# Latent attention with two heads in one pass, a residual kept in DRAM, and index keys on the raw input

## The chip, the cores and the metric

The kernel runs on one core of a Trainium2 chip. A core has five engines that run their own lists of instructions and wait for each other by semaphores: TensorE (PE, matmuls; its weight loads are listed as PEld), VectorE (DVE), ScalarE (ACT), GpSimd (POOL) and SyncE (SP, which only issues DMA here). The metric is the device time of one execution in microseconds (us); less is better.

## The reference, cut to what matters

Two blocks run one after the other on x of 512 tokens by 1024 features, in float32. The first holds an mLSTM, an attention whose keys are selected by an indexer, and a gated embedding. The second holds a state-space mixer (SSD), a latent attention of 16 heads, a gated sum of the two, and a feed-forward part. The change lies in the indexer's key projection, in the residual of the second block, and in the latent attention:

```python
u = rmsnorm(h, norm_in[i])
proj = u @ w_in[i]              # ix_q, ix_k (indexer) are columns of it
...
q = (rms_norm(q_a, q_a_norm_g) @ w_uq).reshape(b, l, MLA_HEADS, MLA_QK_DIM)       # 16 x (64 + 32)
kv = (rms_norm(kv_a, kv_a_norm_g) @ w_ukv).reshape(b, l, MLA_HEADS, MLA_NOPE + MLA_V_DIM)   # 16 x (64 + 64)
k_nope, v = jnp.split(kv, [MLA_NOPE], axis=-1)
k_rope = jnp.broadcast_to(k_rope_raw[:, :, None, :], (b, l, MLA_HEADS, MLA_ROPE))
k = jnp.concatenate([k_nope, k_rope], axis=-1)
q = rms_norm(q, q_norm_g)
k = rms_norm(k, k_norm_g)
...                             # the 32 rope features of q and k are rotated
s = jnp.einsum('bqhd,bkhd->bhqk', qb, k).astype(jnp.float32) * scale              # causal
p = jax.nn.softmax(s, axis=-1).astype(v.dtype)
o = jnp.einsum('bhqk,bkhd->bqhd', p, v)
...
g_ssd, g_mla = jnp.split(jax.nn.sigmoid(gates + gate_b[i]), 2, axis=-1)
x = x + (g_ssd * y_ssd + g_mla * y_mla) @ w_o[i]
```

## The kernel before, in words

Features lie on the 128 partitions and the 512 tokens on the free axis. Every dense product is made of three matmuls for each 128 by 128 part of a weight, because operands are split in a high and a low part (`column_tile`, L678 to L680: high by high, high by low, low by high; 512 columns each). Weights come in chunks of 512 KB, each of eight parts, through a ring of four: SP loads a chunk into `w_raw`, ACT makes `w_hi` of it (L1265), POOL makes `w_lo` (L569), PE uses both. The order of the work is written out by hand for each engine, and semaphores tie the engines together. There are eight PSUM banks of 512 columns.

*Index part.* PE projects the index queries (`idx_q`) from `xg`, the raw input times its gain, whose per-token scale is put in afterwards (`query_scaled` on DVE, L1950), then the index keys (`idx_k`) and the tile `small` from `u`, the normalised input. DVE makes `u_val` (L1956), ACT `u_hi` (L1320), DVE `u_lo` (L1875), eight parts of each.

*Before the SSD.* DVE turns `h_res` into the second block's input and residual in eight instructions (L2215), each of which raises `x2_ready`. ACT issues three small loads of constants (L1574), reads the tile `small2` out of PSUM (L1577) and starts the chain of the time steps (L1581 to L1584, two table loads in it), which DVE goes on with (L2236 on), ahead of the convolution's taps (L2223). PE needs the taps of earlier tiles for their PSUM banks to come free.

*Latent attention.* The list `heads` holds the units (head, query block ti), four to a head, in the order of heads. For unit n PE makes the logits of n+2 (`head_logits`, L1142 and L1143, ti+1 blocks of 128 columns), turns the probabilities of n (`head_turn`, L1151), and multiplies those of n-1 with v (`head_values`, L1161): the turned probabilities are the stationary operand (128 columns) and 64 columns of v move. DVE takes the maximum (L2390, L2391); ACT takes the exponential (`head_probs`, L1751) and copies the turned block (`head_turned`, L1759); DVE divides the product by the sum (`head_out`, L2397 and L2399) into `o_tok`, tokens on partitions, which PE turns back to features for each pair of heads (`back`, L1169), with a DVE copy (L2420). For the head after next PE projects queries and keys (`project_queries`, `project_keys`); ACT squares both (L1718, L1723); DVE makes the features (`head_features`, L2363 to L2372); PE sums the squares over features with a column of ones (`query_sums` L1110, `key_sums` L1119), ACT takes the root (`head_norms`, L1733), DVE the reciprocal, PE spreads the key scale over partitions (`key_spread`, L1128) and DVE multiplies (`head_keys`, L2385). Between all this PE works on a tile of the mixing gates for each head (`mix_gate`, eight parts), for which ACT takes a sigmoid (L1742). Exponential, sigmoid and root stand in different table sets, so ACT loads tables between them. The logits use banks 4 and 5, the turned blocks bank 6, the values bank 7, queries and both sums bank 1, keys and their spread bank 2, gates banks 0 and 3.

*After it.* ACT and DVE split the attention's output (`o_hi` L1787, `o_lo`), PE multiplies it with the output weights (`mla_out`, L699 on), then `mix_out` adds to `h_res`.

## Time and profile before

| | |
|---|---|
| runs, us | 1763.4, 1768.36, 1768.3; median 1768.3 |
| profiled execution, us | 1767.63, of which the span is 1765.8 |
| mean granted clock of TensorE | 0.985 |
| busy, share of the span | PE 96%, PEld 77%, DVE 59%, ACT 48%, POOL 36% |
| latent attention, from its first projections to the first matmul of `mla_out` | 1022.7 to 1305.3 |

Start times of the trace count from the start of the span. A matmul of four-byte type on data that is not split appears as two instructions, and neighbours of one line are drawn together as xN; a matmul's printed duration reaches beyond the start of the next one, so the cost of one is the distance between two starts. What stands in brackets is the idle time of the engine before an instruction and what ended it.

### The profile page before, as it was taken

To read this page: it belongs to the slowest core of one execution; us is meant where nothing else is said; L and a number is where in the kernel's file an instruction comes from. 1 tells how busy PE (TensorE), PEld (TensorE's weight loads), DVE (VectorE), ACT (ScalarE), POOL (GpSimd) and SP (SyncE) were. 2 spreads that over 40 slices of the span, in tenths; PEclk is the share of its full clock that TensorE was granted. 3 is DMA by queue.
4 is the path that set the end of the run, shared out by engine and by line. 5 is a ranking of instruction groups with operands and counts; after the bars stand their busy time and mean duration, and the time that the engine had idled before them with its cause. 6 is when DMAs were issued, how large, how long until landed. Compare 5 with 4: busy or idle time off the path is not lost.

```text
span 1765.8 us, 23111 instructions
## 1 busy us (share of the span) xinstructions
PE 1701.7 (96%) x8091; PEld 1356.3 (77%) x8091; DVE 1045.6 (59%) x1646; ACT 855.6 (48%) x1370; POOL 628.7 (36%) x275
## 2 busy tenths in 40 slices
PE   7999899999999899999999999999999999999999
PEld 5688677767788788776677878888878788888887
DVE  6499478677426767677787045555546556655200
ACT  5423366655435454666663246666663244444210
POOL 4244221232444244343453421221234244444442
PEclk9999899999999899999999999999999899999999
DMA  5223212121333133211112311111113233333331
GB/s 194 65 91 96 89 54 61 59 61 60 134 109 97 50 105 99 72 49 48 37 60 73 106 60 37 61 48 37 50 60 107 72 96 95 96 98 100 99 96 60
DMA packets 39834, 138.56 MB, mean 78 GB/s; under 512 B 4664, under 2 KB 5144, under 8 KB 39616
## 3 DMA queue, kind: packets, MB, share of 16 engines
q1 hardware_dynamic: 37600, 131.96, 24.0%
q10 hardware_dynamic: 2144, 5.39, 1.0%
q8 instruction: 58, 0.95, 0.2%
q14 instruction: 32, 0.26, 0.0%
HBM read 135.21 MB, written 2.12 MB: 78 GB/s over the span
## 4 chain that ended last, share of the span: by engine, by line
PE 77%; DVE 12%; ACT 6%; issue 4%; POOL 0%; DVEq 0%; ACTq 0%; POOLq 0%
PE bank L678 15%; PE bank L680 15%; PE bank L679 15%; PE bank L1249 4%; PE bank L1248 4%; PE bank L1247 4%; PE bank L1142 2%; PE bank L729 1%; PE bank L731 1%; PE bank L730 1%; PE bank L818 1%; PE bank L1073 1%; PE bank L1161 1%; PE bank L836 1%; ACT L1742 1%
## 5 line engine op out<-in xcount | busy, mean ns | idle before, releaser
L569 POOL TENSOR_TENSOR w_lo<-w_raw,w_hi 128x1024 fp32r<-128x1024 f32 x243 | 591.1, 2435 | 1098.5 <-ACT w_hi L1265 953.0
L678 PE MATMUL bank<-u_hi,w_hi 128*128 128x512 f32 x784 | 331.3, 423 | 5.9 <-DVE taps L2223 3.2
L1265 ACT ACTIVATE w_hi<-w_raw 128x1024 fp32r<-128x1024 f32 x199 | 209.2, 1055 | 214.8 <-PE bank L680 176.4
L680 PE MATMUL bank<-u_hi,w_lo 128*128 128x512 f32 x784 | 308.8, 394 | 0.0
L679 PE MATMUL bank<-u_lo,w_hi 128*128 128x512 f32 x784 | 308.2, 393 | 0.0
L678 PEld LDWEIGHTS bank<-u_hi,w_hi 128*128 128x128 f32 x784 | 148.9, 190 | 65.3 <-issue 29.5
L680 PEld LDWEIGHTS bank<-u_hi,w_lo 128*128 128x128 f32 x784 | 148.5, 189 | 32.4
L679 PEld LDWEIGHTS bank<-u_lo,w_hi 128*128 128x128 f32 x784 | 149.2, 190 | 28.4 <-issue 3.1
L1248 PE MATMUL bank<-u_lo,w_hi 128*128 128x512 f32 x320 | 124.5, 389 | 0.0
L1247 PE MATMUL bank<-u_hi,w_hi 128*128 128x512 f32 x320 | 124.5, 389 | 0.0
L1249 PE MATMUL bank<-u_hi,w_lo 128*128 128x512 f32 x320 | 124.5, 389 | 0.0
L1248 PEld LDWEIGHTS bank<-u_lo,w_hi 128*128 128x128 f32 x320 | 60.1, 188 | 12.6
L1247 PEld LDWEIGHTS bank<-u_hi,w_hi 128*128 128x128 f32 x320 | 60.1, 188 | 12.5
L1249 PEld LDWEIGHTS bank<-u_hi,w_lo 128*128 128x128 f32 x320 | 60.1, 188 | 12.4
L2510 DVE TENSOR_TENSOR h_res<-h_res,bank 128x512 f32<-128x512 f32 x8 | 5.5, 687 | 107.1 <-PE bank L680 107.1
L679 PE MATMUL bank<-act_lo,w_hi 128*128 128x512 f32 x176 | 68.5, 389 | 0.0
L678 PE MATMUL bank<-act_hi,w_hi 128*128 128x512 f32 x176 | 68.5, 389 | 0.0
L680 PE MATMUL bank<-act_hi,w_lo 128*128 128x512 f32 x176 | 68.5, 389 | 0.0
L2223 DVE SCALAR_TENSOR_TENSOR taps<-bank,vecs,taps 128x511 f32<-128x511 f32 (+2 forms) x72 | 53.8, 748 | 23.5 <-ACT taps L1619 21.8
L2474 DVE SCALAR_TENSOR_TENSOR ffn_g<-bank,vecs,ffn_g 128x511 f32<-128x511 f32 x22 | 16.5, 750 | 69.5 <-ACT ffn_g L1812 69.5
L678 PE MATMUL bank<-y_hi,w_hi 128*128 128x512 f32 x128 | 51.4, 402 | 3.1 <-DVE y_lo L1875 3.1
L2399 DVE TENSOR_SCALAR o_tok<-bank,x_cols 128x64 f32<-128x64 f32 x64 | 18.1, 284 | 60.8 <-PE bank L1161 60.3
(454 smaller groups left out, 3655.8 us busy)
## 6 DMA issues: line engine op xcount, KB each, us to landing
w_raw<-weights SPq DMA_DIRECT2D x243, 512.0 KB, 3.5
xt<-x_t SPq DMA_DIRECT2D x8, 256.0 KB, 6.2
hank<-bias_dram ACTq DMA_DIRECT2D x8, 256.0 KB, 3.1
xt<-x_t ACTq DMA_DIRECT2D x1, 2048.0 KB, 9.4
out<-h_res SPq DMA_DIRECT2D x8, 256.0 KB
p_val<-p_t ACTq DMA_DIRECT2D x1, 512.0 KB, 11.5
trig<-trig ACTq DMA_DIRECT2D x1, 256.0 KB, 3.9
vecs<-vecs ACTq DMA_DIRECT2D x1, 214.0 KB, 4.8
```

The lines of the kernel that those rows point to most:

```text
L569: pool.tensor_tensor(w_lo[:, j, :], w_raw[:, j, :], w_hi[:, j, :].bitcast(F32), ALU.subtract).then_inc(w_lo_ready, 1)
L678: pe.matmul(o, hi, xh, start=(i == 0), stop=False)
L679: pe.matmul(o, hi, xl, start=False, stop=False)
L680: mm = pe.matmul(o, lo, xh, start=False, stop=(i == n - 1))
L729: pe.matmul(o, xh, hi, start=(k == 0), stop=False)
L1142: pe.matmul(o[:, 0:W], q_s[:, h % 2, ti * P:W], k_s[:, h % 2, 0:W], start=True, stop=False)
L1247: pe.matmul(bank[j][:, :], hi, xh, start=(k == 0), stop=False)
L1248: pe.matmul(bank[j][:, :], hi, xl, start=False, stop=False)
L1249: mm = pe.matmul(bank[j][:, :], lo, xh, start=False, stop=(k == KD - 1))
L1265: act.activation(w_hi[:, c % RING, :], w_raw[:, c % RING, :], ACT.Copy).then_inc(w_hi_ready, 1)
L2223: ins = dve.scalar_tensor_tensor(acc[:, back:S], b[:, 0:S - back], w(n - 1 - back), acc[:, back:S], ALU.mult, ALU.add)
L2399: dve.tensor_scalar(o_tok[:, ti, h * VD:(h + 1) * VD], bank[7][:, 0:VD], x_cols[:, 3, n:n + 1], None, ALU.mult).then_inc(x_out, 1)
```

## The change

1. *Order of units.* `heads` goes over pairs p of heads, query blocks ti, and the two heads s of the pair: the units of two heads alternate. In the loops, i = n mod 8 is the place of a unit in its pair.
2. *Values.* `pair_values` takes both heads of a pair: v (64 columns) is the stationary operand, in the array's column half s, and 128 columns of turned probabilities move. The output lies with features on partitions in bank 7, so `back`, its copy and `o_tok` go; `o_raw` is copied once for each pair. The division by the sum goes ahead of the turn: `head_scaled` (DVE: reciprocal, and a multiplication of the probabilities in place) stands between `head_probs` and `head_turn`.
3. *Keys.* The 64 key features of both heads form one tile of 128 columns (three matmuls for a pair), ACT moves the second head's 64 weight columns beside the first's (a copy in `split_weights`), the key sums take two columns, the spread goes by column halves, and DVE adds the rope part (`key_sums_add`). All sums are now in bank 2, where the keys also are, so `query_sums` of the pair's first head waits until DVE has read the keys (`key_features`).
4. *Gates.* The sigmoid becomes a tanh, with a half in `y_ssd` and in the probabilities, and one added where the gate is used.
5. *Residual.* `h_res` (2 MB) is written to DRAM by ACT's queue after `x2_ready` has come eight times, and read back after the last values; `mix_out` waits for it (`h_back`). Its place in SBUF holds `probs_x` and `turned_x`, four buffers each.
6. *Index keys.* `idx_k` is computed on `xg` as `idx_q` is, and DVE scales it; `u_val` takes the scale from PSUM (bank 5) instead of `r_in` in SBUF.

```diff
+                if k == 6:
+                    pe.wait_ge(ones_ready, 1)
+                    token_sums(lambda k: sq[:, 0, :], lambda k: sq[:, 1, :])
+            column_tile(q2, of_xg, part=(0, 1))
             spread_scale(0, 5)
-            column_tile(q2, of_xg, part=(4, 8))
+            column_tile(q2, of_xg, part=(1, 8))
             column_tile(q3, of_xg)
+            column_tile(st["idx_k"][0], of_xg)
...
-            column_tile(st["idx_k"][0], of_u, 0)
-            column_tile(st["small"][0], of_u)
+            column_tile(st["small"][0], of_u, 0)
...
+            def project_keys(p):
...
+                hi, lo = (w[:, c % RING, 2 * P:3 * P] for w in (w_hi, w_lo))
+                o = bank[2][:, :]
+                pe.matmul(o, hi, kn_hi[:, :], start=True, stop=False)
+                pe.matmul(o, hi, kn_lo[:, :], start=False, stop=False)
+                pe.matmul(o, lo, kn_hi[:, :], start=False, stop=True).then_inc(dense_done, 1)
...
             def query_sums(h):
-                pe.wait_ge(head_sq, 2 * h + 1)
-                pe.wait_ge(dve_freed, st["head_q"][h]["freed"][1])
+                p, s = divmod(h, 2)
+                pe.wait_ge(head_sq, 3 * p + (3 if s else 1))
+                if not s:
+                    pe.wait_ge(head_sq, 3 * p + 2)
+                    pe.wait_ge(dve_freed, st["head_k"][p]["freed"][1])
...
+                    mm = pe.matmul(bank[2][:, s * NT + ti:s * NT + ti + 1], sq_q[:, ti * P:(ti + 1) * P],
+                                   ones[0:QK, 0:1], start=True, stop=True)
+                mm.then_inc(head_sums, 1)
...
+            def key_spread(p):
+                pe.wait_ge(r_qk_ready, p + 1)
...
-                                   stop=True)
+                    for s in range(2):
+                        q = 2 * (NT + c) + s
+                        mm = pe.matmul(bank[2][64 * s:64 * s + 64, c * P:(c + 1) * P],
+                                       r_qk[:, p % 2, q:q + 1].broadcast_to([P, NOPE]), ident[:, :], start=True,
+                                       stop=True)
                 mm.then_inc(rk_spread, 1)
...
-                pe.wait_ge(x_probs, n + 1)
+                pe.wait_ge(x_scaled, n + 1)
...
+            def pair_values(k):
+                p, ti = divmod(k, NT)
+                pe.wait_ge(x_turned_out, 2 * k + 2)
+                if p and ti == 0:
+                    pe.wait_ge(x_out, p)
                 for j in range(ti + 1):
-                    mm = pe.matmul(o, turned_x[n % 2][:, j * P:(j + 1) * P], v_tok[:, j, h * VD:(h + 1) * VD],
-                                   start=(j == 0), stop=(j == ti))
+                    for s in range(2):
+                        h = 2 * p + s
+                        mm = pe.matmul(bank[7][64 * s:64 * s + 64, ti * P:(ti + 1) * P],
+                                       v_tok[:, j, h * VD:(h + 1) * VD],
+                                       turned_x[:, (2 * k + s) % 4, j * P:(j + 1) * P], start=(j == 0), stop=(j == ti))
                 mm.then_inc(x_sum, 1)
...
+                if more and i == 0:
+                    project_query(2 * p + 2)
+                    project_keys(p + 1)
+                if more and i == 2:
+                    project_query(2 * p + 3)
+                if more:
+                    column_tile(st["mix_gate"][2 * p + 1 + i // 4], of_u2, part=(i % 4 * 2, i % 4 * 2 + 2))
+                else:
+                    column_tile(st["mix_gate"][2 * p + 1], of_u2, part=(i, i + 1))
+                if more and i == 1:
+                    query_sums(2 * p + 2)
+                    key_sums(p + 1)
+                if more and i == 3:
+                    query_sums(2 * p + 3)
+                if more and i == 4:
+                    key_spread(p + 1)
...
-                if n:
-                    head_values(n - 1)
...
+                if n and n % 2 == 0:
+                    pair_values(n // 2 - 1)
+            pair_values(len(heads) // 2 - 1)
...
+            act.wait_ge(x2_ready, KD)
+            act.dma_start(h_dram, h_res[:, :, :].rearrange("p a b -> p (a b)")).then_inc(h_spilled, 16)
...
-            act.activation(sq_k[NOPE:QK, :], small2[NOPE:QK, :], ACT.Square).then_inc(krope_sq, 1)
+            act.wait_ge(h_spilled, 16)
...
-                act.activation(gm[:, h % KD, :], bank[t["bank"]][:, :], ACT.Sigmoid,
-                               bias=vec("gate_b", h)).then_inc(act_freed, 1)
+                act.activation(gm[:, h % KD, :], bank[t["bank"]][:, :], ACT.Tanh, bias=half_b[:, h:h + 1],
+                               scale=0.5).then_inc(act_freed, 1)
...
+                if more and i == 0:
+                    query_squares(2 * p + 2)
+                    key_squares(p + 1)
+                if more and i == 2:
+                    query_squares(2 * p + 3)
                 head_turned(n)
-                if ti == 1 and h:
-                    after(st["mix_gate"][h - 1])
-            act.wait_ge(o_turned, KD - 1)
+                if more and i == 2:
+                    after(st["head_q"][2 * p + 3])
+                if more and i == 3:
+                    head_norms(p + 1)
+                    after(st["mix_gate"][2 * p + 1])
+                if more and i == 7:
+                    after(st["mix_gate"][2 * p + 2])
+            act.wait_ge(x_sum, len(heads) // 2)
+            act.dma_start(h_res[:, :, :].rearrange("p a b -> p (a b)"), h_dram).then_inc(h_back, 16)
...
+                act.activation(o_hi[:, i, :], o_raw[:, i, :], ACT.Copy).then_inc(hi_ready, 1)
...
-                return dve.scalar_tensor_tensor(u_val[:, i % 2, :], xt[:, i, :], vec("norm_in", i), r_in[:, :],
+                if i in (4, 6):
+                    query_scaled(i // 2)
+                return dve.scalar_tensor_tensor(u_val[:, i % 2, :], xt[:, i, :], vec("norm_in", i), bank[5][:, :],
...
+            t = st["idx_k"][0]
+            dve.wait_ge(dense_done, t["full"])
+            free(dve.tensor_tensor(ik[:, :], bank[t["bank"]][:, :], r_in[:, :], ALU.mult))
...
+            def key_features(p):
...
+                dve.wait_ge(head_sq, 3 * p + 2)
+                if p:
+                    dve.wait_ge(k_ready, 2 * p)
+                free(dve.tensor_scalar(k_raw[:, :], bank[2][:, :], k_gain[:, :], None, ALU.mult))
...
+            def head_scaled(n):
...
+                W = (heads[n][1] + 1) * P
                 dve.wait_ge(x_probs, n + 1)
                 link(dve.reciprocal(x_cols[:, 3, n:n + 1], x_cols[:, 2, n:n + 1]))
-                dve.wait_ge(x_sum, n + 1)
-                dve.tensor_scalar(o_tok[:, ti, h * VD:(h + 1) * VD], bank[7][:, 0:VD], x_cols[:, 3, n:n + 1],
-                                  None, ALU.mult).then_inc(x_out, 1)
+                dve.tensor_scalar(probs_x[:, n % 4, 0:W], probs_x[:, n % 4, 0:W], x_cols[:, 3, n:n + 1], 0.5,
+                                  ALU.mult, ALU.mult).then_inc(x_scaled, 1)
...
+                head_scaled(n)
+                if p and i == 1:
+                    dve.wait_ge(x_sum, NT * p)
+                    dve.tensor_copy(o_raw[:, p - 1, :], bank[7][:, :]).then_inc(x_out, 1)
+                if more and i == 4:
+                    head_scales(p + 1)
                 if n + 2 < len(heads):
                     head_max(n + 2)
...
+                if more:
+                    if i == 0:
+                        query_features(2 * p + 2, 0)
+                        query_features(2 * p + 2, 1)
+                    if i == 1:
+                        key_features(p + 1)
+                    if i == 2:
+                        key_sums_add(p + 1)
+                        query_features(2 * p + 3, 0)
+                    if i == 3:
+                        query_features(2 * p + 3, 1)
+                    if i in (4, 5):
+                        head_keys(2 * p + i - 2)
+                if i == 2 and 2 * p < KD:
+                    gate_used(2 * p)
+                if i == 5 and 2 * p + 1 < KD:
+                    gate_used(2 * p + 1)
             dve.wait_ge(gates_used, KD)
+            dve.wait_ge(x_sum, len(heads) // 2)
```

On ACT, between the end of the first block and the SSD stage, the list before reads (`u_hi` is the split input, `small_140` the tile `small2`):

```order
L1320 ACTIVATE u_hi<-val_f 128x512 [waits val_ready] x8
L1574 DMA one_hot<-one_hot 96x32
L1574 DMA trig<-trig 128x512
L1574 DMA tri_b<-tri_b 128x128
L1577 ACTIVATE small_140<-bank,vecs 128x512 [waits dense_done]
L1265 ACTIVATE w_hi<-w_raw 128x1024 [waits dense_done,w_landed0]
L1581 ACTIVATE r_t_149<-small_140 32x512 [waits act_freed]
```

and after the change:

```order
L1354 ACTIVATE u_hi<-val_f 128x512 [waits val_ready] x8
L1600 DMA h_dram<-h_res 128x4096 [waits x2_ready]
L1603 DMA one_hot<-one_hot 96x32
L1603 DMA trig<-trig 128x512
L1603 DMA tri_b<-tri_b 128x128
L1606 ACTIVATE small_140<-bank,vecs 128x512 [waits dense_done]
L1299 ACTIVATE w_hi<-w_raw 128x1024 [waits dense_done,w_landed0]
L1610 ACTIVATE r_t_149<-small_140 32x512 [waits act_freed]
```

One DMA with a wait has come in ahead of all the others; nothing else moved.

On PE, in the latent attention, the sums of squares stood in the middle of a head like this (`qn`: the split latent queries, `u`: those of the gates, `squares_f`: the identity):

```order
L1110 MATMUL bank<-ones,sq_q 128x1 [waits dve_freed,head_sq]
L1110 MATMUL bank<-ones,sq_q 128x1 x3
L678 MATMUL bank<-u_hi,w_hi 128x512 [waits w_lo_ready]
L679 MATMUL bank<-u_lo,w_hi 128x512
L680 MATMUL bank<-u_hi,w_lo 128x512
L1119 MATMUL bank<-ones,sq_k 128x1 [waits head_sq]
L1119 MATMUL bank<-ones,sq_k 128x1 x3
L1151 MATMUL bank<-squares_f,probs_x 128x128 [waits x_turned_out,x_probs]
L1161 MATMUL bank<-v_tok,turned_x_180 128x64 [waits x_out,x_turned_out]
L1161 MATMUL bank<-v_tok,turned_x_180 128x64 x3
```

and stand after the change in the second unit of a pair, behind that pair's gate parts:

```order
L694 MATMUL bank<-u_hi,w_hi 128x512
L695 MATMUL bank<-u_lo,w_hi 128x512
L696 MATMUL bank<-u_hi,w_lo 128x512
L1148 MATMUL bank<-ones,sq_q 128x1 [waits dve_freed,head_sq]
L1148 MATMUL bank<-ones,sq_q 128x1 x3
L1156 MATMUL bank<-in_half,sq_k 128x2 [waits head_sq]
L1156 MATMUL bank<-in_half,sq_k 128x2 x3
L1190 MATMUL bank<-squares_f,probs_x 128x128 [waits x_turned_out,x_scaled]
L1181 MATMUL bank<-k_s,q_s 128x384 [waits x_probs]
L1182 MATMUL bank<-tri_b,squares_b 128x128
```

The sums of the first query and of the keys now follow each other without a matmul of the gates between them, the first of them waits for DVE's reading of the keys, and the turn behind them waits for `x_scaled` (DVE) where it waited for `x_probs` (ACT).

On ACT, around the roots, before (one head):

```order
L1751 ACTIVATE probs_x,x_cols<-bank,x_cols,r_qk 128x256 [waits x_turn,x_max]
L1733 ACT_TABLE_LOAD [waits rk_spread,x_probs]
L1733 ACTIVATE r_qk<-bank,vecs 128x4 [waits head_sums]
L1734 ACTIVATE r_qk<-bank,vecs 128x4
L1759 COPY turned_x_179<-bank 128x128 [waits x_sum,x_turn]
L1742 ACT_TABLE_LOAD
L1742 ACTIVATE gm<-bank,vecs 128x512 [waits dense_done]
L1751 ACT_TABLE_LOAD [waits x_turn]
L1751 ACTIVATE probs_x,x_cols<-bank,x_cols,r_qk 128x384 [waits x_max]
```

and after (fourth to fifth unit of a pair):

```order
L1787 COPY turned_x<-bank 128x256 [waits x_turn]
L1759 ACT_TABLE_LOAD [waits k_sums_in]
L1759 ACTIVATE r_qk<-bank,vecs 128x8 [waits head_sums]
L1760 ACTIVATE r_qk<-r_qk,vecs 128x8
L1299 ACTIVATE w_hi<-w_raw 128x1024 [waits dense_done,w_landed0]
L1769 ACT_TABLE_LOAD
L1769 ACTIVATE gm<-bank,half_b 128x512 [waits dense_done]
L1779 ACTIVATE probs_x,x_cols<-bank,x_cols,r_qk 128x384 [waits x_turn,x_max]
L1787 COPY turned_x<-bank 128x384 [waits x_sum,x_turn]
```

Two of the three table loads are still there, now once for a pair of heads; the load between gate and exponential is gone; a weight copy stands between root and gate.

## Rows read from the trace of the kernel before

**Rows 1.** The page, its first part: busy time, share and count of each engine.

```profile
PE 1701.7 (96%) x8091; PEld 1356.3 (77%) x8091; DVE 1045.6 (59%) x1646; ACT 855.6 (48%) x1370; POOL 628.7 (36%) x275
```

**Rows 2.** Windows of the latent attention: us, busy (count), PEclk, DMA share, GB/s.

```profile
1022.70:1038.40 15.70, 15.70 (x83) 13.38 (x82) 7.16 (x11) 7.70 (x13) 2.39 (x1) 1.00 0.17 61
1038.40:1304.80 266.40, 260.83 (x1556) 214.50 (x1554) 145.49 (x377) 178.71 (x340) 57.14 (x24) 0.97 0.15 47
1042.20:1049.00 6.80, 5.85 (x22) 4.59 (x23) 2.49 (x6) 3.80 (x8) 4.23 (x2) 0.62 0.43 131
```

**Rows 3.** Groups of instructions by line and form, 1000 to 1320 us.

```profile
L1751 ACT ACT_TABLE_LOAD x17 | 21.8, 1283 | 0.3
```

**Rows 4.** Timeline of PE inside one head: start, us, engine, line.

```profile
1178.88 0.39 PE L680 MATMUL bank<-u_hi,w_lo 128*128 128x512 f32 x1
1179.11 0.95 PE L1119 MATMUL bank<-ones,sq_k 96*128 96x1 f32 x8
1179.92 0.31 PE L1151 MATMUL bank<-squares_f,probs_x 128*128 128x128 f32 x1
1180.07 1.00 PE L1161 MATMUL bank<-v_tok,turned_x 128*128 128x64 f32 x8
1180.91 0.65 PE L1142 MATMUL bank<-k_s,q_s 96*128 96x512 f32 x1
```

**Rows 5.** Timeline of PE in the SSD stage, column halves.

```profile
740.97 0.38 PE L969 MATMUL bank<-squares_b 128*128 128x512 bf16 x1
741.28 0.41 PE L979 MATMUL bank<-stack_a,one_hot 96*64 96x512 bf16 x2
741.66 0.51 PE L1073 MATMUL bank<-weight_a,xdt 128*64 128x128 f32 x3
```

**Rows 6.** Waits of PE, 1020 to 1320 us.

```profile
PE bank L1110 <- DVE q_s L2368: 2.2, 2, 1.6
```

**Rows 7.** Timeline of DVE: the features of one head.

```profile
1173.64 0.73 DVE L2363 TENSOR_SCALAR q_s<-bank,vecs 64x512 f32<-64x512 f32 x1
...
1176.70 0.74 DVE L2372 TENSOR_SCALAR rope<-bank,vecs 64x512 f32<-64x512 f32 x1
```

**Rows 8.** Timeline of ACT: a table load, a gate, a weight copy.

```profile
1164.20 1.28 ACT L1742 ACT_TABLE_LOAD   x1
1165.50 0.69 ACT L1742 ACTIVATE gm<-bank,vecs 128x512 f32<-128x512 f32 x1
...
1173.89 1.05 ACT L1265 ACTIVATE w_hi<-w_raw 128x1024 fp32r<-128x1024 f32 x1
```

**Rows 9.** Timeline of POOL in the index part.

```profile
41.24 2.52 POOL L569 TENSOR_TENSOR w_lo<-w_raw,w_hi 128x1024 fp32r<-128x1024 f32 x1 [2.24 <-ACT w_hi L1265]
```

**Rows 10.** Timeline of DVE in the index part.

```profile
40.18 0.75 DVE L1956 SCALAR_TENSOR_TENSOR u_val<-xt,vecs,r_in 128x512 f32<-128x512 f32 x1
...
41.57 2.75 DVE L1956 SCALAR_TENSOR_TENSOR u_val<-xt,vecs,r_in 128x512 f32<-128x512 f32 x1
```

**Rows 11.** One line, L2012, DVE: duration min/median/max.

```profile
L2012 DVE TENSOR_SCALAR relu<-score,top x3: 420/487/2485, 142.2 to 155.9; 128x256 f32<-128x256 f32 x1, 128x384 f32<-128x384 f32 x1, 128x512 f32<-128x512 f32 x1
```

**Rows 12.** Timeline of PE in the index part.

```profile
44.97 0.50 PE L678 MATMUL bank<-u_hi,w_hi 128*128 128x512 f32 x1 [2.29 <-DVE u_lo L1875]
...
48.67 0.63 PE L678 MATMUL bank<-u_hi,w_hi 128*128 128x512 f32 x1
```

**Rows 13.** Timeline of ACT before the SSD stage.

```profile
587.37 1.65 ACTq L1574 DMA_DIRECT2D trig<-trig  x1
...
591.69 0.69 ACT L1577 ACTIVATE small<-bank,vecs 128x512 f32<-128x512 f32 x1 [4.06 <-PE bank L704]
```

**Rows 14.** Timeline of DVE at the same place.

```profile
592.81 5.36 DVE L2215 SCALAR_TENSOR_TENSOR h_res<-h_res,vecs,bank 128x512 f32<-128x512 f32 x8 [4.39 <-PE bank L654]
...
609.12 2.97 DVE L2223 SCALAR_TENSOR_TENSOR taps<-bank,vecs,taps 128x511 f32<-128x511 f32 x4
```

**Rows 15.** Timeline of PE at the same place.

```profile
611.49 0.50 PE L678 MATMUL bank<-u_hi,w_hi 128*128 128x512 f32 x1 [2.39 <-DVE taps L2223]
```

More of the change, by code:

```diff
@@ L133, in make_plan @@
     plan = Plan()
-    for name, n, kt, reader in (("idx_q", 4, KD, "D"), ("idx_k", 1, KD, "A"), ("small", 1, KD, "A"),
+    for name, n, kt, reader in (("idx_q", 4, KD, "D"), ("idx_k", 1, KD, "D"), ("small", 1, KD, "A"),
                                 ("att_q", 4, KD, "A"), ("att_k", 4, KD, "A")):
@@ L469, in weight @@
             return weights2[h // 2 % 2][:, h % 2, :]
-        heads = [(h, ti) for h in range(XH) for ti in range(NT)]
+        heads = [(2 * p + s, ti) for p in range(XH // 2) for ti in range(NT) for s in range(2)]
         up = st["up"]
@@ L1256, in _ @@
             next_hi, steps, evs, sqs, his = [0], [0], [0], [0], [0]
+            pair_chunks = [t["parts"][0][0] for t in st["head_k"]]
             def split_weights(done):
@@ L1359, in _ @@
             token_std(bank[4][:, 0:NT], 0)
-            for i, t in enumerate(st["idx_q"]):
+            for t, first, end in zip(st["idx_q"] + st["idx_k"], (0, 0, 3, 5, 7), (0, 3, 5, 7, KD)):
                 tile_done(t)
                 after(t)
-                if i:
-                    n = (3, 2, 3)[i - 1]
-                    k = (0, 3, 5)[i - 1]
-                    high_parts(lambda i: u_hi[:, k + i, :], lambda i: u_val[:, (k + i) % 2, :], n)
+                high_parts(lambda i: u_hi[:, first + i, :], lambda i: u_val[:, (first + i) % 2, :], end - first)
             act.wait_ge(bias_dot, 1)
@@ L1376, in _ @@
             act.sem_inc(bias_ready, 1)
-            t = st["idx_k"][0]
-            tile_done(t)
-            act.copy(ik[:, :], bank[t["bank"]][:, :]).then_inc(act_freed, 1)
-            after(t)
             t = st["small"][0]
@@ L2442, in fuse @@
+            low(bank[7][:, :], o_hi[:, KD - 1, :], o_lo[:, KD - 1, :])
             def fuse(i):
```

371 lines of the change are left out of this document (182 added, 189 removed).

## The prediction

> **What bounds the kernel now.** I read the page's first part, then the latent attention by windows, then PE's waits there, then the timelines of single heads. PE is busy 96% of the span, the other engines 36 to 59% [rows 1], so an edit pays by the PE time that it removes and costs by the PE wait that it adds. The latent attention takes 15.7 us of preparation and 266.4 us of loop, together 282.1, with PE idle 5.6 of it and a mean granted clock of 0.97 in the loop [rows 2]. PE's only long waits there are for DVE's query features, 2.2 us in two [rows 6]. After the first of them the clock stood at 0.62 for 6.8 us, half speed for most of it [rows 2]; so an idle moment of PE costs more than its length. At 260.8 busy us, 3% of clock is 7.8 us at most; I take 6.8. Full-clock PE work of the stage is then 282.1 - 5.6 - 6.8 = 269.7.
>
> **PE work that goes.** Keys: three 512-column matmuls for a pair instead of six, 24 fewer at 0.23 each (1178.88 to 1179.11) [rows 4], 5.5 us. Key sums: 4 columns of 4 matmuls for each pair instead of 8 matmuls; eight instructions take 0.81 (1179.11 to 1179.92) [rows 4], so 8 x 0.81 = 6.5, with the change-over 7.2. Spread: 64 matmuls of 96 stationary columns become 64 of 64 columns in alternate halves. Values: 160 matmuls, 320 instructions, at 0.84 for eight (1180.07 to 1180.91) [rows 4] = 33.6; their number stays, but neighbours now go to different column halves. Two 512-column products in two column halves both stand at 741.28, and the next instruction starts 0.38 later, where one alone takes 0.23 and two would take 0.46 [rows 4, 5]. So halves run beside each other, and a change of form costs some 0.09 going in (0.31 from 740.97 to 741.28) and coming out. The floor is then half the price: values 33.6/2 and spread (priced as the sums, 16 x 0.81 = 13) 13/2, a gain of 16.8 + 6.5, and 1.8 for the short units. The other end of the range is no overlap at all: gain nothing, and 0.1 in and 0.1 out of each group. I take the overlap, as the nearest row in form shows it. Switches: five groups for a pair (four of values, one of spread) and the last, 41 x 0.19 = 7.8 back. Turning back goes: 32 matmuls, at 0.11 each (0.81 for eight) [rows 4] 3.5. Sum: 5.5 + 7.2 + 25.1 + 3.5 - 7.8 = 33.5 less, 236.2 left.
>
> **Waits that come.** Worked through one pair of the new order with the old durations, PE meets five. (a) In the second unit `query_sums` stands behind logits, query, keys and two gate parts, about 7.0 us after the pair's start, and needs the keys read by DVE. ACT has 3.6 us ahead of the squares' end (a turned block, the weight copy 1.05 [rows 8] with the small copy that it follows now, gate, exponential, square), DVE then four query operations, 3.06 us together [rows 7], `head_scaled`, a maximum of 0.65, the copy of the values and the key operation of 0.74 [rows 7], 5.5 in all: 9.1, so PE waits 2.1. Behind the waiting instruction stand the key sums, the turn and the logits; ACT's next roots depend on the sums. (b) In the fourth unit, 0.4, the query features behind one multiplication. (c) In the fifth, 0.5, the spread behind roots and reciprocal. (d) In the same place 1.0: ACT has turned block, table load 1.29, roots, weight copy 1.05, table load, gate 0.69 and exponential in a row [rows 3, 8] before PE's logits buffer comes free. (e) 0.3 for the first values of a unit. Together 4.3 for each of seven pairs, 30.1, and 3.5 in the preparation, where four of these chains run for the first time: 33.6. Table loads fall from 48 (17 in the row shown, 16 and 15 in two like it, 1.28 each [rows 3]) to 15; ACT waited for PE, not PE for ACT, so this pays nothing by itself.
>
> So the stage is 236.2 + 33.6 = 269.8 before the clock. The clock: before, one wait of 1.65 us was followed by the fall [rows 2, 6]; now seven pairs have one of 2.1 beside eight one-column sums. If each fall costs 1.4 us and the preparation 2, the sum is 11.5, between 4 (falls in a few pairs) and 18 (all as deep as the one shown). I take 11.5: 281.3, **0.8 less** than now.
>
> The trace shows 1.30 us from the start of a table load to the activation behind it [rows 8]. The Trainium skill, "ScalarE: Activation LUTs", section "What ACT_TABLE_LOAD costs", adds a drain of some 1.38 us to every load of 1.28. By it wait (d) would be 2.7 us longer for each pair, 19 us in all; the time would be 1794. The trace has no such gap, so the row stands in the sum and that case gets no chance.
>
> **The spill.** ACT's queue now waits for eight `x2_ready` ahead of the other loads and ahead of `small2`. DVE's eight instructions run 592.81 to 598.17; `small2` is read at 591.69 today [rows 13, 14]. It would be read behind 598.17, one issue of 0.34, and the three constants' (1.65 for the longest [rows 13], 2.4 together): 601.1, which is 9.4 later; 8.0 if the long issue shrinks in a quiet queue. The time-step chain behind it (ACT two table loads, DVE until 609.12 [rows 14]) hides nothing: DVE follows ACT closely, then the taps start at 609.12, and PE waits for them already, 2.39 us until 611.49 [rows 15]. So PE starts again at 620.9 and, after 12 us of idling, at half clock for a while, 2 us. Nothing in the SSD stage catches up, since PE had no other wait over 0.2 us in the next 100 us. **11.4 more**, 8 to 14. The transfer itself has hundreds of us.
>
> **The index part.** DVE's `u_val` takes 2.75 us instead of 0.75 where POOL's `w_lo` runs [rows 9, 10]; PE waits 2.29 for it at 44.97, and `small` starts at 48.67 at half clock [rows 12]. Now `idx_k` needs no `u`, and seven of eight parts can be ready behind it; `u_val` with one operand in SBUF shouldn't stretch. `small` would start at 44.4 or so at full clock: 4.2 + 0.8 = **5.0 less**, 3.5 to 6.
>
> **Behind the attention.** `mla_out` starts behind the last values (`x_sum`), the issue of the 2 MB read, and one copy of 0.6, where today most copies lie under the last unit: **1.2 more**. The read itself is needed a whole `mla_out` later.
>
> **Sum.** -0.8 + 11.4 - 5.0 + 1.2 = 6.8 on the profiled execution of 1767.6, which is 0.7 below the median of the runs; I give **1775.0 us** against 1768.3, 0.4% more. Under 0.3% (5.3 us) nothing can be told from no change here.
>
> **The rivals.**
> *A, the forecast*, 1766 to 1784. Chance 0.48.
> *B, the saving reaches the end*: waits (a) to (e) are half of what I worked out (an operation order one step better than mine, or DVE's 59% load [rows 1] leaving room), and the clock stays up. Then 15 us of waits and 9 of clock are saved: 1751, 1743 to 1760. For it: DVE and ACT both lose work. Against it: the sums now wait for DVE's reading of a shared bank. It decides when (a) is below 1 us. Chance 0.22.
> *C, the spill is hidden*: DVE ends its eight instructions sooner or the time steps have slack that I don't see. 11 less, 1764. Against it the 2.39 us wait at 611.49 [rows 15]. Chance 0.08.
> *D, column halves don't overlap* for four-byte operands; the product in rows 5 is of two-byte ones, and four-byte ones in alternate halves (L1073 in the same rows) start 0.05 apart in some places of the SSD stage and 0.11 in others. Of the 3.1 us that the overlap gives for each pair (25.1 / 8) 2.2 would be missing, the rest shortens waits: seven times, 1790. Chance 0.10.
> *E, POOL holds up `head_scaled`*. That operation goes from SBUF to SBUF, as L2012 does, which took 0.42 to 0.49 us and once 2.49 [rows 11]; before, the division read PSUM. It now stands between exponential and turn, three 512 KB chunks for a pair, each with 2.5 us of POOL [rows 9]. If one in each pair is caught fully, 2.0 us, and the 0.4 of wait (b) hides a part, 1.6 reach PE, 11 in seven pairs: 1786. The Trainium skill, "SBUF — State Buffer", section "Who interferes with whom", says the same of such operations: they take a port pair that GpSimd shares, and one fully blocks the other. Chance 0.12.
>
> **How the numbers follow.** Faster: B and the low ends of A and C, 0.30. Within 0.3%: a third of A, half of C, 0.20. Slower: the rest of A, D and E, 0.50. The likeliest case's own range is 1766 to 1784; since cases of both signs hold the chance, the range reaches from 1746 in B to 1790 in D and E, and leaves about 2 in 10 out.
>
> **What would show it.** `small2` read at about 601 and an idle PE of 10 us or more at 609 to 621; PE without its 2.3 us wait at 45; the stage from the first `head_q` to `mla_out` within 4 us of 282; two in-pair waits of 1 to 2 us behind DVE's key operation and ACT's gate, and PEclk at 8 there; pairs of L1202 instructions 0.05 to 0.06 apart (D: 0.11); `head_scaled` at 0.3 to 0.5 us (E: 2 us and more). The prediction is wrong if the attention stage is under 270 us, or if the spill's delay doesn't arrive at PE.

## The result, and the profile after

The changed kernel takes 1785.2 us (1784.8 to 1785.9, 4 runs) against 1765.9 (1760.4 to 1768.4, 4 runs): ratio 1.0114, 95% interval 1.0087 to 1.0142. It is 1.1% slower: the side that was forecast and inside the range (1746 to 1790), but 19 us more instead of 7, and a microsecond outside what the likeliest case allowed (1766 to 1784).

The page of the changed kernel, span, busy shares and the row of the clock, against [rows 1]:

```profile
span 1783.3 us, 22683 instructions
PE 1687.7 (95%) x7960; PEld 1323.6 (74%) x7979; DVE 1069.8 (60%) x1667; ACT 809.7 (45%) x1320; POOL 629.1 (35%) x275
...
PEclk9999899999998899999999989999999999999999
```

PE is busy 14 us less and the span is 17.5 longer, so what was removed is not what decided the time. (The profiled executions, whose spans are compared from here on, differ by 17.5 us, the medians by 19.4.) Four marks of the two traces tell where it goes. ACT's last `u_hi` ahead of the SSD starts at 581.59 instead of 587.00: 5.4 sooner. PE goes on behind the taps at 616.50 instead of 611.49 [rows 15]: 5.0 later, so 10.4 were lost in between. The first query of the latent attention starts at 1029.5 instead of 1022.7, 6.8 later; `mla_out` starts at 1324.2 instead of 1305.3, 18.9 later; the end is 17.5 later. So: index part -5.4, spill (the write of the residual) +12.2, latent attention +12.1, behind it -1.4.

From the first mark on, ACT's queue before the SSD (DMA issues of ACT are marked ACTq), against [rows 13], then PE at the same place, against [rows 15]:

```profile
581.59 0.63 ACT L1354 ACTIVATE u_hi<-val_f 128x512 fp32r<-128x512 f32 x1 [0.75 <-DVE val_f L2254]
593.60 0.33 ACTq L1600 DMA_DIRECT2D h_dram<-h_res  x1
...
595.42 1.29 ACTq L1603 DMA_DIRECT2D tri_b<-tri_b  x1
596.76 0.69 ACT L1606 ACTIVATE small<-bank,vecs 128x512 f32<-128x512 f32 x1 [14.54 <-issue]
```

```profile
600.97 0.47 PE L694 MATMUL bank<-u_hi,w_hi 128*128 128x512 f32 x1 [1.91 <-POOL w_lo L585]
616.50 0.79 PE L694 MATMUL bank<-u_hi,w_hi 128*128 128x512 f32 x1 [9.85 <-DVE taps L2267]
```

ACT sits idle for 14.5 us in front of `small2`. At PE this comes out as two waits: 9.85 for the taps, and 1.91 for a weight chunk whose `w_hi` stands behind `small2` on ACT.

The latent attention by windows, whole and for two pairs of heads (columns as in [rows 2]), then PE's waits in it, against [rows 6]:

```profile
1029.48:1324.18 294.70, 265.01 (x1529) 196.46 (x1528) 175.27 (x401) 140.51 (x302) 59.37 (x25) 0.93 0.15 48
```

```profile
1085.63:1122.11 36.48, 33.05 (x189) 24.55 (x188) 21.19 (x51) 17.11 (x37) 7.12 (x3) 0.91 0.14 44
1122.11:1157.65 35.54, 31.61 (x190) 23.23 (x189) 23.28 (x51) 17.11 (x37) 7.11 (x3) 0.95 0.15 46
```

```profile
PE bank L1148 <- DVE k_raw L2424: 11.6, 7, 1.8
PE bank L1181 <- ACT probs_x L1779: 9.1, 9, 1.2
PE bank L1190 <- DVE probs_x L2463: 2.2, 6, 0.5
PE bank L745 <- DVE v_tok L1959: 1.7, 1, 1.7
PE bank L1166 <- DVE r_qk L2438: 1.5, 7, 0.4
PE bank L1181 <- DVE k_s L2447: 1.5, 2, 0.9
PE bank L715 <- ACT o_hi L1831: 1.3, 1, 1.3
PE bank L1202 <- ACT turned_x L1787: 0.7, 1, 0.7
```

A pair of heads takes 34 to 37 us, where two heads took 33.3 to 34.7 before. The waits come to 29.6 us. PE around one of the longest waits, in the pair from 1122.11:

```profile
1134.91 0.40 PE L696 MATMUL bank<-u_hi,w_lo 128*128 128x512 f32 x1
1137.13 1.02 PE L1148 MATMUL bank<-ones,sq_q 96*128 96x1 f32 x8 [1.82 <-DVE k_raw L2424]
1138.01 1.03 PE L1156 MATMUL bank<-in_half,sq_k 128*128 128x2 f32 x8
...
1140.94 0.63 PE L695 MATMUL bank<-qn_lo,w_hi 128*128 128x512 f32 x1
1141.37 0.63 PE L696 MATMUL bank<-qn_hi,w_lo 128*128 128x512 f32 x1
```

Some two microseconds behind the idle time the matmuls slow down: a 512-column one costs 0.43 instead of 0.23 (1140.94 to 1141.37). This is the lower of the clock's two levels, 1.2 instead of 2.4 GHz, here for 3.4 us. In three pairs it lasts twice as long, behind the same wait of 1.8 us. Two windows inside such stretches, the first in the pair from 1085.63:

```profile
1101.60:1108.30 6.70, 6.70 (x21) 5.23 (x22) 0.84 (x3) 1.31 (x4) 0.00 (x0) 0.50 0.01 2
1139.15:1142.45 3.30, 3.30 (x9) 2.12 (x8) 0.84 (x3) 0.82 (x3) 0.00 (x0) 0.50 0.00 0
```

I call such a stretch a fall of the clock. In the stage there are six falls of 3.4 us and three of 6.8, 41.0 us at half speed together, in which half, 20.5 us, is lost. In the kernel before there were one of 6.8 and two of 3.4: 13.7 us, 6.8 lost.

### The profile page after: what moved, and what is told of

It reads as the page before. It is cut to its first block, busy times and chain, and to the rows that moved or that the text cites. A ratio compares the mean times of both kernels' runs of the same rounds, so it can differ in the third digit from the quotient of the medians.

```text
span 1783.3 us, 22683 instructions
## 1 busy us (share of the span) xinstructions
PE 1687.7 (95%) x7960; PEld 1323.6 (74%) x7979; DVE 1069.8 (60%) x1667; ACT 809.7 (45%) x1320; POOL 629.1 (35%) x275
## 4 chain that ended last, share of the span: by engine, by line
PE 74%; DVE 15%; ACT 6%; issue 4%; POOL 0%; ACTq 0%; DVEq 0%; POOLq 0%
PE bank L694 15%; PE bank L696 14%; PE bank L695 14%; PE bank L1278 4%; PE bank L1277 4%; PE bank L1279 4%; PE bank L1181 2%; PE bank L745 1%; PE bank L746 1%; PE bank L747 1%; PE bank L835 1%; PE bank L1090 1%; PE bank L853 1%; ACT w_hi L1299 1%; PE bank L1190 1%
## 5 line engine op out<-in xcount | busy, mean ns | idle before, releaser
L694 PE MATMUL bank<-u_hi,w_hi 128*128 128x512 f32 x776 | 327.0, 421 | 12.5 <-DVE taps L2267 10.6
L1787 ACT COPY turned_x<-bank 128x128 f32<-128x128 f32 (+3 forms) x64 | 27.3, 426 | 114.0 <-PE bank L1190 114.0
L1279 PEld LDWEIGHTS bank<-u_hi,w_lo 128*128 128x128 f32 x320 | 60.1, 188 | 12.5
L2410 DVE TENSOR_SCALAR q_s<-bank,vecs 64x512 f32<-64x512 f32 x16 | 11.9, 743 | 82.8 <-ACT sq_q L1748 82.8
L2454 DVE TENSOR_REDUCE x_cols<-bank 128x1 f32<-128x128 f32 (+3 forms) x64 | 31.4, 490 | 50.4 <-PE bank L1182 49.6
```

Source lines behind the costliest of these rows:

```text
L694: pe.matmul(o, hi, xh, start=(i == 0), stop=False)
L1279: mm = pe.matmul(bank[j][:, :], lo, xh, start=False, stop=(k == KD - 1))
L1787: act.copy(turned_x[:, n % 4, 0:W], bank[6][:, 0:W]).then_inc(x_turned_out, 1)
L2454: link(dve.reduce_max(x_cols[:, 0, n:n + 1], bank[4 + n % 2][:, 0:(ti + 1) * P], AX_X))
```

## The experiments

Twelve kernels ran, each beside runs of the kernel before on the same chip. Times are medians; ratios are to the kernel before, with 95% intervals.

**1. The index part alone**, on the kernel before (part 6 of the change):

```diff
             column_tile(q3, of_xg)
+            column_tile(st["idx_k"][0], of_xg)
...
-            column_tile(st["idx_k"][0], of_u, 0)
```

> The kernel before with the index part of the change alone. If the index part is worth what the trace of the changed kernel suggests (everything behind it starts 5.4 us sooner), the time falls by 5 to 5.5 us, to 1760.5, with no PE wait at 45 us. If that gain is given back where PE next waits for a chunk of weights or a DVE chain, it falls by less than 2 us.

1758.9 against 1763.9, ratio 0.9973 (0.9958 to 0.9987): 5 us less, where the interval allows 2 to 7. PE has no wait left between 26 and 100 us but one of 0.4. The part does what was forecast.

**2. The residual alone**, written and read back, on the kernel before:

```diff
+            act.wait_ge(x2_ready, KD)
+            act.dma_start(h_dram, h_res[:, :, :].rearrange("p a b -> p (a b)")).then_inc(h_spilled, 16)
...
+            act.dma_start(h_res[:, :, :].rearrange("p a b -> p (a b)"), h_dram).then_inc(h_back, 16)
...
+            dve.wait_ge(h_back, 16)
```

> The kernel before with the residual written out and read back where the change does it, and nothing else. Theory: the wait on ACT's queue alone costs 10 to 12 us (1776 to 1778), with PE idle some 10 us behind the taps. Rival: the wait costs little by itself and the long idle time in the changed kernel comes from the earlier arrival of PE (index part); then the time rises by 4 to 6 us only.

1777.3, ratio 1.0069 (1.0051 to 1.0087): 12 us more by the ratio. PE's waits at the place, in this kernel:

```profile
PE bank L681 <- DVE taps L2230: 9.8, 1, 9.8
PE bank L681 <- POOL w_lo L572: 1.9, 1, 1.9
```

They are those of the changed kernel to a tenth, so neither the index part nor the attention has a share in them.

**3. The changed kernel with the residual written later**, behind the time-step chain:

```diff
-            act.wait_ge(x2_ready, KD)
-            act.dma_start(h_dram, h_res[:, :, :].rearrange("p a b -> p (a b)")).then_inc(h_spilled, 16)
...
             act.activation(r_t2[:, :], r_t2[:, :], ACT.Ln, bias=1.0).then_inc(dt_log, 1)
+            act.wait_ge(x2_ready, KD)
+            act.dma_start(h_dram, h_res[:, :, :].rearrange("p a b -> p (a b)")).then_inc(h_spilled, 16)
```

> The changed kernel with the write of the residual issued behind the time-step chain. The output is unchanged. Theory: 9 to 11 us come back (1785.2 to 1775), the wait behind the taps is 2 to 3 us again. Rival (something else holds the time steps): less than 3 us. Whatever stays above 1766 - 5 = 1761 is then the attention's, 12 to 14 us.

1772.6, ratio 1.0049 (1.0031 to 1.0067), 0.65% below the changed kernel. The wait behind the taps is 2.2 us. So the place of one DMA issue on a queue cost over 11 us; the transfer, which is made here too, costs nothing that shows.

**4. The changed kernel with the keys read first** by DVE:

```diff
                         query_features(2 * p + 2, 0)
                         query_features(2 * p + 2, 1)
-                    if i == 1:
                         key_features(p + 1)
```

> The changed kernel with DVE's reading of the keys moved ahead of a scaling, a maximum and the copy of the values. Theory that waits and the clock falls behind them make the attention slow: the wait for k_raw (11.6 us in 7) falls below 2 us, and falls of the clock go with it; 10 us from the waits and 7 x 1.7 from the clock, 1763 to 1770. Rival, that the clock falls for another reason (one-column sums in one block): the waits go but the falls stay, 1775 to 1777. Rival, that the next wait takes its place (the exponential, 9.1 us in 9): 1780 and more.

1763.7, ratio 0.9996 (0.9983 to 1.0008): 21 us below the changed kernel, the time of the kernel before. The latent attention of this kernel:

```profile
1029.00:1301.20 272.20, 253.55 (x1529) 188.65 (x1528) 174.64 (x401) 140.38 (x302) 59.27 (x25) 0.97 0.17 52
```

The wait for `k_raw` is gone; the others stay as they were (9.1, 2.2, 1.7 and so on; only the one for `r_qk` falls from 1.5 to 1.2). The stage is 22.5 us shorter. Of this 11.0 is idle time (29.7 falls to 18.7), and 11.5 is busy time for the same matmuls, which is the clock: 17.1 us at half speed instead of 41.0. So half of what a 1.8 us wait cost came behind it.

Two of the five falls that are left stand behind the one-column sums with no wait over 0.3 us ahead of them. One of them, and a window of the kernel before with such a fall:

```profile
1129.83 1.03 PE L1156 MATMUL bank<-in_half,sq_k 128*128 128x2 f32 x8
...
1132.00 0.63 PE L695 MATMUL bank<-qn_lo,w_hi 128*128 128x512 f32 x1
1132.43 0.63 PE L696 MATMUL bank<-qn_hi,w_lo 128*128 128x512 f32 x1
```

```profile
1146.30:1149.50 3.20, 3.20 (x7) 1.74 (x8) 1.19 (x3) 3.16 (x4) 0.00 (x0) 0.50 0.00 0
```

**5. The sums apart**, in the changed kernel: a gate part between query sums and key sums.

```diff
-                if more:
+                if more and i == 1:
+                    column_tile(st["mix_gate"][2 * p + 1], of_u2, part=(2, 3))
+                elif more:
...
                     query_sums(2 * p + 2)
+                    column_tile(st["mix_gate"][2 * p + 1], of_u2, part=(3, 4))
                     key_sums(p + 1)
```

> The changed kernel (no repair) with one gate part moved between the query sums and the key sums, so that the one-column matmuls behind the wait no longer stand in one block; the wait for the keys stays and grows by 0.7 in each of seven pairs. Theory that idleness makes the clock fall: the falls (40.9 us at half speed) stay, the time is that of the changed kernel or up to 5 us more. Rival, that the block of one-column matmuls is what lets it fall: the falls go, 8 to 12 us less.

1795.6, ratio 1.0175 (1.0161 to 1.0189), 11 us above the changed kernel. Its latent attention:

```profile
1027.36:1333.20 305.84, 272.14 (x1530) 201.82 (x1528) 173.17 (x401) 140.54 (x302) 59.41 (x25) 0.91 0.15 46
```

The wait for `k_raw` grew from 11.6 to 16.1 us and the falls from 41.0 to 58.0 us at half speed, though the one-column matmuls no longer stand in a block. So in these kernels the falls grow and shrink with the idle time, and parting the sums doesn't take them away. Idle time isn't their only cause: the falls without a wait in number 4 and in the kernel before stand behind such sums, and what makes those was not tested. The time went up by more than the 5 us of either theory, because I had not let the falls grow with the wait.

**6. Three repairs together**: late residual, keys first, and on ACT the fifth unit's gate and its weight copy behind the exponential.

```diff
-                if more and i == 4:
-                    mix_gate(2 * p + 1)
                 if n + 1 < len(heads):
                     head_probs(n + 1)
+                if more and i == 4:
+                    after(st["mix_gate"][2 * p + 1])
...
+                if more and i == 4:
+                    mix_gate(2 * p + 1)
                 if more and i == 3:
                     head_norms(p + 1)
-                    after(st["mix_gate"][2 * p + 1])
```

> The changed kernel with three repairs: the residual written behind the time steps, the keys read first, and ACT's gate and weight copy of the fifth unit behind the exponential. If the first two add up (12.7 and 21.5 us, from the same changed kernel's 1785.2), 1751; the third takes most of the 9.1 us for which PE waits for the exponential, so 1743 to 1748. If that wait only moves (to the turned blocks or the next gate's bank), 1750 to 1752. Against 1764 of the kernel before: ratio 0.988 to 0.993.

1757.0, ratio 0.9958 (0.9944 to 0.9971), above what was expected of two repairs alone. PE's wait for the exponential fell from 9.1 to 1.5, and one for the scaling rose from 2.2 to 12.9. DVE and POOL there, in this kernel:

```profile
1134.28 0.16 DVE L2463 RECIPROCAL x_cols<-x_cols 128x1 f32<-128x1 f32 x1
1134.48 2.61 DVE L2464 TENSOR_SCALAR probs_x<-probs_x,x_cols 128x384 f32<-128x384 f32 x1
```

```profile
1134.49 2.38 POOL L585 TENSOR_TENSOR w_lo<-w_raw,w_hi 128x1024 fp32r<-128x1024 f32 x1 [5.23 <-ACT w_hi L1299]
```

The moved weight copy lets POOL start as the scaling does, in almost every pair: 11 of 64 scalings take over 1 us, where it was 4 in the changed kernel, and 0.42 is usual for 384 columns.

**7. The two repairs without the third.**

> The changed kernel with two repairs: the residual written behind the time steps, and the keys read first. If the two add up (12.7 and 21.5 us) 1751, ratio 0.992 to the kernel before. The kernel with the third repair as well measured 1757; if that third one was harmful because it put POOL's weight copies on the scaling (11 scalings stretched instead of 4), this kernel is 3 to 6 us faster than it and has 4 stretched scalings. Rival, that the two repairs don't add up: 1757 here too.

1753.3, ratio 0.9937 (0.9918 to 0.9957). Five scalings over 1 us. The two repairs bring 1.8% in ratio against the changed kernel, where alone they bring 0.65 and 1.2: they add up. That the third was harmful is likely from this but not certain, since the intervals of numbers 6 and 7 overlap (0.9944 to 0.9971 against 0.9918 to 0.9957).

**8. Two repairs, and the gate alone behind the exponential** (the weight copy stays where it was):

```diff
-                if more and i == 4:
-                    mix_gate(2 * p + 1)
                 if n + 1 < len(heads):
                     head_probs(n + 1)
...
+                if more and i == 4:
+                    mix_gate(2 * p + 1)
                 if more and i == 3:
                     head_norms(p + 1)
                     after(st["mix_gate"][2 * p + 1])
```

> The two repairs (late residual, keys first; 1753.3, ratio 0.9937), and of the third only the gate's tanh moved behind the exponential and the turned block; the weight copy stays between root and table load. The exponential comes 0.6 us sooner, when POOL's w_lo (from 0.1 us after the weight copy, 2.4 us long) is all but over. Theory that only the moved weight copy made the third repair harmful: the waits for the exponential fall from 8.9 to 3 to 5 us, no more than 6 scalings take over 1 us, the time falls by 3 to 6 us to 1747 to 1750. Rival, that any earlier exponential meets POOL: 10 or more stretched scalings, 1754 or more.

1749.1 (1744.1 to 1753.1), ratio 0.9919 (0.9899 to 0.9938): the fastest kernel of the study whose output is whole, 0.8% under the kernel before. Its waits:

```profile
PE bank L1181 <- ACT probs_x L1779: 4.9, 9, 1.2
PE bank L1190 <- DVE probs_x L2463: 2.7, 7, 0.5
```

Five scalings over 1 us. This kernel and that of number 6 differ in the weight copy's place alone, and their intervals lie apart (0.9899 to 0.9938 against 0.9944 to 0.9971): that place did the harm.

**9. The scaling with an odd number of columns**, on the kernel with three repairs and, as a second run, on that with two:

```diff
-                dve.tensor_scalar(probs_x[:, n % 4, 0:W], probs_x[:, n % 4, 0:W], x_cols[:, 3, n:n + 1], 0.5,
+                dve.tensor_scalar(probs_x[:, n % 4, 0:W - 1], probs_x[:, n % 4, 0:W - 1], x_cols[:, 3, n:n + 1], 0.5,
+                                  ALU.mult, ALU.mult)
+                dve.tensor_scalar(probs_x[:, n % 4, W - 1:W], probs_x[:, n % 4, W - 1:W], x_cols[:, 3, n:n + 1], 0.5,
                                   ALU.mult, ALU.mult).then_inc(x_scaled, 1)
```

> The kernel with three repairs, with each scaling of the probabilities cut into two instructions, of all columns but the last and of the last, so that the long one has an odd number of columns; the result is the same. Theory that the scaling in its even form waits for GpSimd's port: none of the 64 takes over 1 us, where 11 took up to 2.6; the waits for it fall from 12.9 to under 4 us, the time from 1757 to 1743 to 1748. Rival, that it is blocked whatever its form: 11 stretched ones stay, and the second instruction adds up to 10 us.

> Two repairs (late residual, keys first) and the odd scaling. If POOL's hold is worth little here (4 stretched scalings), the second instruction costs as much as it saves: the same as with two repairs, 1749 to 1752. If it frees ACT's and DVE's order, 1745.

1758.1, ratio 0.9973 (0.9959 to 0.9987), and 1755.9, ratio 0.9957 (0.9942 to 0.9972): no gain in either; 13 and 6 stretched scalings. The odd form takes the same time as the even one (medians of 0.421 and 0.420 for 383 columns beside 0.421 for 384) and is caught just as often. My theory that an odd count takes the scaling out of POOL's way fell. The Trainium skill, "VectorE: DVE Perf Modes", section "Mode 2×_2P — use both read ports for one tensor", asks of the mode in which DVE reads one tensor through both of its read ports that the outermost dimension be even, or odd and equal in source and destination, as it is here; I had read over the second half, and the trace agrees with it.

**10. No scaling**, on the kernel with three repairs; the output lacks the division by the sum:

```diff
-                link(dve.reciprocal(x_cols[:, 3, n:n + 1], x_cols[:, 2, n:n + 1]))
-                dve.tensor_scalar(probs_x[:, n % 4, 0:W], probs_x[:, n % 4, 0:W], x_cols[:, 3, n:n + 1], 0.5,
-                                  ALU.mult, ALU.mult).then_inc(x_scaled, 1)
+                dve.reciprocal(x_cols[:, 3, n:n + 1], x_cols[:, 2, n:n + 1]).then_inc(x_scaled, 1)
```

> The kernel with the three repairs and without the multiplication of the probabilities (the reciprocal stays; the output lacks the division by the sum). It tells what it costs to have the division between exponential and turn. From the waits that name it (2.2 us) 2 to 4 us; if it also holds back everything on DVE behind it, and POOL stretches it, 8 us or more.

1738.8, ratio 0.9863 (0.9847 to 0.9878): 18 us under number 6, far more than the 2 to 4 of the small guess and in the 8 or more of the other. The whole of the 12.9 us wait goes. It bounds what the place of the division is worth in that kernel; in number 8, where the wait is 2.7, it must be much less, which was not run.

**11. Neighbours in the same column half**, on the kernel with three repairs: all blocks of one head, then all of the other.

```diff
-                for j in range(ti + 1):
-                    for s in range(2):
+                for s in range(2):
+                    for j in range(ti + 1):
```

> The kernel with the three repairs, but the values of one head made wholly before those of the other, so that neighbours go to the same column half; the work is the same. Theory that neighbours in different halves overlap: instructions of this line start 0.11 apart instead of 0.06, 160 matmuls cost 320 x 0.05 = 16 us more, less a few us that waits absorb: 10 to 16 us slower. Rival, that the column form alone is fast: no change.

1756.4, ratio 0.9953 (0.9935 to 0.9971): no change. The longest group in number 6, where the heads alternate, then in this kernel, with the instruction behind it:

```profile
1247.39 1.09 PE L1202 MATMUL bank<-turned_x,v_tok 128*64 128x128 f32 x16
1248.41 0.70 PE L1181 MATMUL bank<-k_s,q_s 128*128 128x256 f32 x2
```

```profile
1248.53 1.58 PE L1202 MATMUL bank<-turned_x,v_tok 128*64 128x128 f32 x16
1250.05 0.70 PE L1181 MATMUL bank<-k_s,q_s 128*128 128x256 f32 x2
```

Sixteen take 1.02 in alternate halves and 1.52 one after the other, so the overlap is real; but groups of four and eight take the same in both orders (0.37 and 0.6). The values of the whole stage take 28.5 us instead of 22.4, so the overlap is worth 6 us, where I expected 10 to 16. Only 2.4 of them show in the stage (279.5 against 277.1); 1.7 are hidden by the clock, which stood at half speed for 13.7 us here and 17.1 in number 6.

## Why the prediction was right and where it was wrong

The terms of the latent attention are compared in work at full clock, idle time and clock. The stage's 282.6 us before hold 270.1, 5.6 and 6.8 of them; its 294.7 after hold 244.5, 29.7 and 20.5. Work is what is left when idle time and half of the time at half speed are taken off.

*Index part.* -5.0 forecast, -5.4 in the trace, -5 alone: right, by its own step.

*Spill.* +11.4 forecast; 12.2 in the trace, 12 alone. `small2` and with it PE's restart were forecast 9.4 late and came 10.5 and 10.4 late; DVE's eight instructions start at 588.2, 4.6 sooner than in [rows 14] and not 5.4, which is most of the difference. Another 1.8 are lost behind the restart, at half speed as forecast (2). I had not seen the wait for `w_lo`; it lies ahead of the one for the taps, which would only have been longer without it. Rival C falls.

*Waits in the attention.* 33.6 forecast, and 1.2 behind the attention; 29.7 of idle time in the trace, of which 1.3 is the wait for `o_hi` that the forecast counts behind it. Wait (a) was forecast at 2.1 and is 1.8 at most, 11.6 in seven; (d) 1.0 and is 1.2 at most; (b), (c) and (e) are as small as forecast. That step was right in what PE waits for, and 5 us too high in all.

*The clock.* This is the first step that failed in size: 11.5 forecast, 20.5 measured, above even the 18 of its upper end. It priced a fall at 1.4 us. (Seven such and 2 for the preparation are 11.8, not 11.5.) The row that it went by stood at 0.62 for 6.8 us [rows 2], which is a loss of 2.6, and no reason was given for taking half of that. The short falls lose 1.7 each, and three last 6.8 us and lose 3.4. Number 4 shows that 11.5 of the loss hang on wait (a), and number 5 that it grows with it.

*PE work.* This is the second: 33.5 less forecast, 25.6 less measured (270.1 to 244.5; number 4, with other waits, has 245.0). Distances between starts, weighted with the clock, tell where the 8 us are missing. Keys (5.7 less, 5.5 forecast), turning back (3.5) and the spread with its switches (4.6, some 4.8 forecast) came out. Two terms did not:

- The values, switches in, were to give 12.5 (16.8 and 1.8 less 6.1) and give 8.0. Their own instructions fell nearly as forecast, from 34.5 to 22.9, but the turns ahead of them rose from 18.0 to 21.6, since the change-over is paid there: four of them take 0.56 on average ahead of the values and 0.44 ahead of logits, where they took 0.44 ahead of the values before.
- The sums were to give 7.2 and give 4.1. Those of the keys fell from 13.0 to 7.2, but those of the queries, which now stand next to them, rose by 0.7, and the new sums of the rope part take 1.0, for which nothing was set down.

A group of turns and the values behind it, before and after:

```profile
1139.62 0.60 PE L1151 MATMUL bank<-squares_f,probs_x 128*128 128x128 f32 x4
1140.06 0.78 PE L1161 MATMUL bank<-v_tok,turned_x 128*128 128x64 f32 x6
```

```profile
1232.28 0.60 PE L1190 MATMUL bank<-squares_f,probs_x 128*128 128x128 f32 x4
1232.81 0.88 PE L1202 MATMUL bank<-turned_x,v_tok 128*64 128x128 f32 x12
```

*Behind the attention.* 1.2 more forecast; the wait for `o_hi` is 1.3, and lies ahead of the first matmul of `mla_out`, so it is part of the attention's 12.1. The stretch behind that mark is 1.4 shorter. The change has no share in this that the trace shows: at its one fall of the clock before the last microseconds, in both kernels at the norm ahead of the feed-forward part, the clock stood at half speed for 10.2 us before (from 1395.4) and 6.8 after (from 1415.6), which is 1.7 us. The kernels of numbers 3 and 4 have 10.2 there again, those of 7 and 8 have 6.8.

Sum of the steps: 5.4 down, 12.2, 12.1 and -1.4 up, 17.5. In the attention the work was 7.9 short of the forecast and the clock 9.0 over it, while the waits were 5.1 under it; so the sign came out right by the spill and the index part, which were priced right, and the size missed by 11 us because the attention's saving was eaten up. The sign that I had set, a stage within 4 us of 282, failed: it took 294.7. That the time still lies inside the range is in part luck, because its upper end was set for rivals D and E, and neither came. Rival B needed wait (a) to be below 1 us: that is number 4, where the condition is made true, and the attention comes out 22.5 us shorter, close to the 24 that the rival promised. Rival D fell (number 11). Rival E's mechanism exists but was rare in the changed kernel, 4 of 64; the repair of number 6 made it common.

## What to carry to other kernels

Where an engine's queue is written by hand, price a wait by what stands behind it on that queue: one DMA issue ahead of a small activation cost 12 us, and its transfer nothing. On a busy TensorE look at the clock's row before counting removed matmuls: here a wait of up to 1.8 us that came back in every pair cost twice its length, and moving one DVE instruction ahead of a scaling, a copy and a maximum was worth 21 us. Price a group of short matmuls together with what stands next to it, since a change of form can be paid by the neighbour. After a repair, list the waits again: the engine that is let go sooner may meet another, as the scaling met POOL.

## What the runs showed of the hardware that I had not expected

- Short recurring waits of PE bring the clock down: with seven waits of up to 1.8 us it stood at half speed for 41.0 us of the stage, with up to 2.5 us for 58.0, and without them for 17.1, though PE's nine waits of up to 1.2 us for the exponential were still there. A wait of the same 1.8 us was followed by a fall of 3.4 us in some pairs and of 6.8 in others, and some falls of 3.4 us came with no wait over 0.3 us ahead.
- A DVE multiplication from SBUF to SBUF that starts together with POOL's `w_lo` takes 2.61 instead of 0.42 us, with an odd column count as with an even one.
- With `u_val` reading PSUM the stretch went to the next DVE instruction with two SBUF operands (`u_lo`, 1.5 to 2.4 us instead of 0.7), where other work hid it.
- Of the groups of 4, 8, 12 and 16 instructions with 64 stationary columns, only those of 12 and 16 are faster in alternate halves of the array than in one half after the other (0.81 against 1.07 and 1.02 against 1.52 us; 0.37 and 0.6 in both orders for 4 and 8).
